# Reordering a two-layer hybrid decoder step: first stage by sets of chunks, pages and weights a stage ahead, linear attention without GpSimd products, key copies ahead of scalings

## The reference

```python
x = layer_norm(x)                                   # 1088 rows of 1024
for l in range(2):
    shift1, scale1, gate1, shift2, scale2, gate2 = split(silu(c) @ w_ada[l] + b_ada[l], 6)   # 9 rows c
    h = x * (1 + scale1) + shift1
    gq, gk, gv, gg, glr, lx, lgate, dq, dkv, kr = split(h @ w_in[l])
    o_gla = rms_norm(gla(gq, gk, gv, log_sigmoid(glr @ w_gate + b) / 16)) * silu(gg)   # chunked linear attention
    o_lru = gelu(lgate) * rg_lru(causal_conv(lx))                                      # a scan over the tokens
    q = rms_norm(dq) @ w_uq; q_lat = q_nope @ w_uk                                     # latent attention, 8 heads
    keys = concat(past_ckv[page_table], rms_norm(dkv)), concat(past_kr[page_table], rope(kr))
    o_mla = softmax(q_lat @ keys_c.T + rope(q_rope) @ keys_r.T, causal) @ keys_c @ w_uv
    x = layer_norm(alpha * x + gate1 * (concat(o_gla, o_lru, o_mla) @ w_out[l]))
    h2 = x * (1 + scale2) + shift2
    x = layer_norm(alpha * x + gate2 * ((silu(h2 @ w_g) * (h2 @ w_u)) @ w_down))
```

## Time and profile before

| | |
|---|---|
| median of 3 runs | 3480.62 us (3478.95 to 3488.6) |
| the profiled execution, its own time | 3485.3 us |
| its span, first to last instruction | 3483.5 us |
| TensorE busy | 3255.1 us (93%) |
| VectorE busy | 2326.5 us (67%) |
| ScalarE busy | 1587.2 us (46%) |
| GpSimd busy | 202.9 us (6%) |
| mean granted TensorE clock | 0.966 |

### The profile page before, as it was taken

How to read it: one execution, slowest core, us unless ns; L and a number is a source line. 1 busy time by engine, 2 the same in 40 slices (tenths; PEclk the granted TensorE clock), 3 DMA queues, 4 the chain that set the end, 5 groups by cost and what they waited for, 6 DMA issues and landing times. The chain is left out here.

```text
span 3483.5 us, 61376 instructions
## 1 busy us (share of the span) xinstructions
PE 3255.1 (93%) x23676; PEld 2738.1 (79%) x23676; DVE 2326.5 (67%) x4390; ACT 1587.2 (46%) x3159; POOL 202.9 (6%) x254
## 2 busy tenths in 40 slices
PE   6988898998999999999989889989989999999997
PEld 4875566776998998999978655667769899899997
DVE  5254665444488889888844456644446888888878
ACT  5343554444255454444344445634433554544432
POOL 0020111110000000000001111011100000000000
PEclk9998999998999999999989889999989999999998
DMA  7026102443033332222121340044421333322231
GB/s 272 27 93 230 66 1 105 164 157 106 16 106 96 95 101 80 90 87 86 52 109 31 137 142 1 1 163 165 158 49 52 94 98 96 94 87 83 91 106 57
DMA packets 158149, 334.72 MB, mean 96 GB/s; under 512 B 18556, under 2 KB 85406, under 8 KB 146471
## 3 DMA queue, kind: packets, MB, share of 16 engines
q1 hardware_dynamic: 146342, 246.91, 22.2%
q0 software_dynamic: 11520, 83.89, 6.8%
HBM read 315.32 MB, written 15.43 MB: 95 GB/s over the span
## 5 line engine op out<-in xcount | busy, mean ns | idle before, releaser
L2494 ACT CAST w_ffn_hi<-w_ffn 128x512 fp32r<-128x512 f32 x616 | 371.3, 618 | 259.4 <-DVE w_ffn L2676 128.0
L445 PE MATMUL psum<-h_lo,w_ffn_hi 128*128 128x256 f32 (+1 forms) x1408 | 406.6, 289 | 0.0
L2688 DVE TENSOR_TENSOR w_ffn_lo<-w_ffn,w_ffn_hi 128x1024 fp32r<-128x1024 f32 (+1 forms) x366 | 383.0, 1047 | 11.8 <-ACT w_ffn_hi L2494 11.7
L444 PE MATMUL psum<-h_forms_hi,w_ffn_hi 128*128 128x288 f32 x1232 | 364.1, 296 | 3.4 <-DVE w_ffn_lo L2688 3.4
L446 PE MATMUL psum<-h_forms_hi,w_ffn_lo 128*128 128x288 f32 x1232 | 363.7, 295 | 0.0
L444 PE MATMUL psum<-h_hi,w_ffn_hi 128*128 128x256 f32 x1232 | 348.6, 283 | 10.9 <-DVE w_ffn_lo L2688 9.1
L444 PE MATMUL psum<-ffn_act_hi,w_down_hi 128*128 128x288 f32 (+1 forms) x992 | 332.3, 335 | 21.1 <-DVE w_down_lo L2694 6.5
L446 PE MATMUL psum<-h_hi,w_ffn_lo 128*128 128x256 f32 x1232 | 346.8, 281 | 0.0
L446 PE MATMUL psum<-ffn_act_hi,w_down_lo 128*128 128x288 f32 (+1 forms) x992 | 326.6, 329 | 0.0
L445 PE MATMUL psum<-ffn_act_lo,w_down_hi 128*128 128x288 f32 (+1 forms) x992 | 325.9, 328 | 0.0
L430 DVE SCALAR_TENSOR_TENSOR xT<-psum,adaT,xT 128x512 f32<-128x512 f32 (+2 forms) x320 | 191.1, 609 | 130.4 <-PE psum L446 127.0
(11 more groups left out here) (450 smaller groups left out, 7624.8 us busy)
## 6 DMA issues: line engine op xcount, KB each, us to landing
w_ffn<-in_w_gu SPq DMA_DIRECT2D x352, 256.0 KB, 2.6
w_ada_pair<-in_w_ada SPq DMA_DIRECT2D x40, 1024.0 KB, 6.1
w_down<-in_w_down SPq DMA_DIRECT2D x192, 192.0 KB, 2.4
residual_kept<-xT SPq DMA_DIRECT2D x2, 4352.0 KB, 19.2
xT<-residual_kept SPq DMA_DIRECT2D x2, 4352.0 KB, 14.2
w_ada_first<-in_w_ada SPq DMA_DIRECT2D x4, 2048.0 KB, 22.2
w_out<-in_w_out SPq DMA_DIRECT2D x16, 512.0 KB, 7.3
w_in_T<-in_w_in_T SPq DMA_DIRECT2D x12, 512.0 KB, 4.4
```

Of the source, the lines that this page charges most:

```text
L444: pe.matmul(o, wh, xh, start=first, stop=False)
L445: pe.matmul(o, wh, xl, start=False, stop=False)
L2494: act.copy(WGH[:, (j + 1) % NR].bitcast(F32R), WGR[:, m % 2, i]).then_inc(s_wh, 1)
L2688: dve.tensor_tensor(WGL[:, m % 2, i:i + n].bitcast(F32R), WGR[:, m % 2, i:i + n], WGH[:, r:r + n], ALU.subtract).then_inc(s_wl, n)
```

## The change

Start and input: the transposes run column group by column group and start when three row blocks are normalised, through four banks; the weights of the modulation come in 1 MB loads so that each set j holds shift and scale of chunks 2j and 2j+1, and vectors and modulation go set by set. Most of the constants are loaded, and the page indices computed, in the input stage. `w_in_B` is loaded in the stage before (in layer 1: at the end of layer 0's feed-forward part), and in layer 0 the split of k = 0 is made there too.

```diff
+            gg = [(c, n) for n in range(3) for c in range(KD)]
+            def back_bank(g):
+                return bank(4 + g % 4)
...
                     for j, (g0, g1) in enumerate(STAGES):
+                        pe.wait_ge(nm, min(NBLK, 3 * j + 3))
                         for g in range(g0, g1):
                             back(g)
+                            if j and g == g0 + 3:
+                                rows_turned(j - 1)
+                        ada(j)
+                    rows_turned(2)
+                    ada(3)
+                    rows_turned(3)
...
+                    sp.wait_ge(tb, len(gg))
+                    for k in range(KD):
+                        sp.dma_start(WBR[:, k], of("w_in_B", 0)[:, k]).then_inc(s_wb[k > 0], 16)
...
-                    for k in range(KD):
+                    for k in range(k_0, KD):
+                        act.copy(wbh(k).bitcast(F32R), WBR[:, k]).then_inc(s_bh, 1)
                         act.copy(HIN[:, k].bitcast(F32R), HT[:, k]).then_inc(s_hh, 1)
-                        act.wait_ge(s_wb[k], 16)
-                        act.copy(wbh(k).bitcast(F32R), WBR[:, k]).then_inc(s_bh, 1)
```

```diff
-        ADA_PER_STEP = {24: (1, 2, 3, 3, 3, 3, 3, 3, 2, 1), 16: (1, 2, 2, 2, 2, 2, 2, 2, 1, 0)}
+        ADA_PER_STEP = {24: (2, 3, 3, 3, 3, 3, 3, 2, 1, 1), 16: (2, 2, 2, 2, 2, 2, 2, 1, 1, 0)}
+        MIXED_AT = (2, 3)
...
-                    for c in range(2):
-                        pool.tensor_tensor(HT[:, 2 + c], LG[:, c], XC[:, c], ALU.mult).then_inc(s_mx, 1)
...
+                            for q in todo[:1] if s == 1 else ():
+                                pair(q)
                             if s + 1 < NBLK:
                                 cumulate(s + 1)
-                            for q in todo[:1]:
+                            for q in todo[:1] if s > 1 else ():
                                 pair(q)
                             attend(s - 1)
...
+                        if s in MIXED_AT:
+                            c = MIXED_AT.index(s)
+                            dve.tensor_tensor(HT[:, 2 + c], LG[:, c], XC[:, c], ALU.mult).then_inc(s_mx, 1)
```

```diff
-            for hp in range(1, HP):
-                for j in range(NPJ):
-                    pj_at.setdefault((hp - 1) * PER + 5 + j, []).append((hp, j))
+            SPREAD = {hp: (5, 8, 9, 10, 11, 12, 13, 14, 15, 16) if hp == 1 else (1, 4, 5, 8, 9, 10, 12, 13, 14, 15)
+                      for hp in range(1, HP)}
+            for hp, at_items in SPREAD.items():
+                for j, x in enumerate(at_items):
+                    pj_at.setdefault((hp - 1) * PER + x, []).append((hp, j))
...
+                    page_rows(pool, 0).then_inc(s_pf, 16)
+                    rope_rows(pool, 0).then_inc(s_pf, 16)
...
+                        for hp, j in pj_at.get(i, []) if i > 4 else ():
+                            read(hp * NPJ + j)
                         if i:
                             scale(i - 1)
...
-                        for hp, j in pj_at.get(i, []):
+                        for hp, j in pj_at.get(i, []) if i <= 4 else ():
                             read(hp * NPJ + j)
```

```diff
+                @block.sync
+                def _(sp):
+                    sp.wait_ge(s_v, NS - 2)
+                    sp.wait_ge(s_s, NS - 1)
+                    for k in range(NPRE):
+                        sp.dma_start(wo(k)[0][:, 0:KD - 1], w_out_rows(k)[:, 0:KD - 1]).then_inc(s_ow[k], 16)
...
                     keys(0)
-                    pe.wait_ge(s_na, 1)
+                    new_turned()
                     pe.wait_ge(s_ql, 1)
-                    for s in range(NS):
+                    for s in range(NS - 1):
                         scores(s)
-                        if s + 1 < NS:
-                            keys(s + 1)
+                        if s == 0:
+                            new_values()
+                        keys(s + 1)
...
-                    values(NS - 1)
+                    scores(NS - 1)
+                    values(NS - 2)
                     pe.wait_ge(s_mx, NS)
                     pe.transpose(bank(0)[0:SB, 0:P], NMR[:, :, NCH], ident).then_inc(s_fp, 1)
+                    turn(NS - 1)
...
+                    values(NS - 1)
                     pe.wait_ge(s_f, 3)
```

```diff
                     for k in range(KD):
-                        pe.wait_ge(s_xl, k + 1)
-                        pe.wait_ge(s_ol, k + 1)
+                        if k:
+                            pe.wait_ge(s_xl, k)
+                            pe.wait_ge(s_ol, k)
...
-                            act.wait_ge(s_om, 3 * KD if j == NR - 1 else 2 * KD)
-                        act.copy(WGH[:, (j + 1) % NR].bitcast(F32R), WGR[:, m % 2, i]).then_inc(s_wh, 1)
+                            act.wait_ge(s_om, (2 * KD, KD + 10, KD + 10, KD + 12, KD + 12, 3 * KD)[j])
+                        act.copy(WGH[:, (j + 1) % NR].bitcast(F32R), wg(WGR, m, i)[:, 0]).then_inc(s_wh, 1)
```

More of the change, by code:

```diff
@@ L599, in t_end @@
                 return at_item[("T", j, 2)] + 1
-            s_wb = [sem(f"w_in_B_{k}_in") for k in range(KD)]
+            s_rest = sem("consts_in")
+            k_0 = 1 if layer[0] == 0 else 0
+            s_fa = sem("first_pairs_in")
             s_wa, s_wt, s_p = sem("w_in_A_in"), [sem(f"w_in_T_{i}_in") for i in range(3)], sem("params_in")
@@ L1002, in _ @@
                         scan(c)
+                    for b in range(SB if layer[0] == 0 else 0):
+                        dve.tensor_scalar(IDX[:, b, 0:NCH], bc(PT[:, b], NCH), float(2 * NCH), None, ALU.mult)
+                        lk(dve.tensor_scalar(IDX[:, b, NCH:NCH + 1], PT[:, b:b + 1], 2.0, None, ALU.mult))
+                        lk(dve.tensor_tensor(IDX[:, b, :], IDX[:, b, :], IBASE, ALU.add))
                 @block.gpsimd
@@ L1071, in stage_gla @@
             s_az = sem("ada_bank_zero")
-            pairs = range(M_G1 // 2 if layer[0] == DEPTH - 1 else 0, ADA_PAIRS)
+            pairs = ada_pairs()
             PARTS = [(0, 4), (4, 7), (7, NBLK)]
@@ L2188, in build, with wg, wo, wo_hi @@
         assert C_SM + 4 + 2 * D <= C_N
+        def wg(parts, m, i, n=1):
+            i0, _, w = next(x for x in parts[m % 2] if x[0] <= i and i + n <= x[1])
+            return w[:, i - i0:i - i0 + n]
+        def wo(k):
+            return WOR[:, k // 4, :, k % 4], WOL[:, k // 4, :, k % 4]
+        def wo_hi(k):
+            return WOH[:, :, k]
+        def w_out_rows(k):
+            return of("w_out")[:, k].rearrange("p (c n) -> p c n", n=P)
         def row_in_h(blk):
```

472 lines of the change are left out of this document (289 added, 183 removed).

## The result

The changed kernel takes 3391.86 us (median of 4 runs, 3388.07 to 3396.17), the one before 3479.78 us beside it: a ratio of 0.9744, 95% interval 0.9721 to 0.9766, 88 us less where 68 were forecast. Run again later it took 3383.35 us (5 runs), ratio 0.9718 (0.970 to 0.9736). The result lies inside the forecast range (3382 to 3446), 20 us under the forecast of 3412, and at the figure of the clock rival, 3391. Its profiled execution has a span of 3394.1 us, of which TensorE is busy 3231.4 (95%).

What follows compares the result with a forecast made beforehand. TensorE, busy 93% of 3483.5 us, was taken as the bound, so only its idle or lower-clock time could be won. Seam by seam savings summed to 68.4 us, taking the 3480.6 median to 3412, range 3382 to 3446.

Steps and rivals of the forecast that it cites:

- the clock rival: Whole kernel, mainly linear attention: fewer holes also mean fewer stretches at 1.2 GHz, 21 us more, 3391 us; chance 0.19.
- The sum: Whole kernel: seam by seam savings, 7 + 0.9 + 14 + 16 + 14 + 16.5 = 68.4 us.
- Start and input, 7 us: First stage to first input product: early transposes, modulation by sets, weights ready; 8.4 less 1.4, range 5 to 9.5.
- the early transposes: First stage: half a block of transposes moves ahead, before all rows are normalised, saving 2 us.
- Linear attention, 7 each: Each layer: without GpSimd's products beside VectorE, the 6.8 us hole shrinks to about 1.3; 7 us, range 1 to 16.
- 1.6 in each: Linear attention, each layer: some 1.6 us of doubled time at the lower clock behind the hole shrinks with it.
- Prompt attention, 8 each: Each layer: key and query copies ahead of ScalarE's scaling, with spread positions, remove TensorE's waits; 8 us, range 0 to 12.
- The prompt rival: Prompt attention gives nothing, as scaling and turn are late in place of the copy; 3428 us, chance 0.14.
- Entry and exit of decode, 10.9 each: Decode, each layer: 7 us at the entry and 3.9 from the shortened chain and split copies at the tail.
- the 7 forecast: Entry to decode, each layer: prefetched page keys first, new values behind the scores; 7 us, range 4 to 9.
- the 10.3: Exit from decode and output stage, layer 0: shorter tail and output weights and split made ahead; range 8 to 12.
- Output stage, 6.4 and 2.3: Output product: 6.4 us in layer 0 from weights and split ahead, 2.3 in layer 1 from splits after the gains.

Runs made afterwards that it cites:

- one: Changed kernel with the two gate-by-scan products of linear attention back on GpSimd and off VectorE; 3393.76 us, ratio 0.9755.
- three: Changed kernel with ScalarE's reads of the projections behind the scaling again in prompt attention, positions still spread; 3397.1 us, ratio 0.9742.
- four: Changed kernel with prompt attention's projections at their old steps 5 to 14, ScalarE still reading them ahead of the scaling; 3397.94 us, ratio 0.9754.
- seven: Changed kernel with page 0 and its rope rows fetched at the start of the decode stage again; 3402.74 us, ratio 0.9776.
- eight: Changed kernel with w_out 0 to 3 loaded and the k = 0 operands split in the output stage again; 3398.58 us, ratio 0.976.
- run two: Kernel before, with only the two gate-by-scan products of linear attention moved from GpSimd to VectorE; 3459.84 us, ratio 0.9942.
- eleven: Changed kernel with the first stage's small turning products late and no-effect products in linear attention's two 1.3 us holes and four further places; 3372.7 us, ratio 0.9701.
- ten: Kernel before, with 24 small extra products of no effect in linear attention's 6.8 us hole; 3475.0 us in 11 runs, ratio 0.9981.

## Why the prediction was right, and where it was off

**The sum.** 68.4 us forecast, 65.7 and 68.0 us of idle time saved. The sum was right as a sum over holes, and off as a forecast of the time because it counted 3 us for the clock, which gave 21 and 35.

**Start and input, 7 us.** Idle time fell by 8.6 and 7.0 us, the early transposes by their 2.7. The term was right for the holes, but the lower clock, for which I took off 1.4 with the kept rows, cost 9.8 us more than before in the first profile and 2.9 in the second. In runs one, three, four, seven and eight, which share this stage, the linear stage began at 231.7 to 232.5 us, 6 us earlier than the 238.2 of before, against 237.3 and 235.3 in the two profiles of the changed kernel.

**Linear attention, 7 each.** The step is right: 5.56 to 1.17 us, hole 1.39 (1.3 forecast). The first of the 1.29 us products is hidden: it runs at 253.75, in a stretch (250.0 to 266.7) in which TensorE is busy 16.70 of 16.70 us. Idle time saved 7.5 and 6.0 in the first profile. What failed is the size of the clock's part: in layer 1 15.8 and 13.0 us came back in the two profiles, in layer 0 -1.5 and 4.7, against 1.6 in each. In layer 1 all eleven profiles with the new order of pairs lost 2.7 to 9.7 us, the two with the old order and the products on GpSimd 17.4 and 18.9, and run two 7.8; in layer 0 they scatter on both sides of before (4.9 to 19.8 against 9.5 to 11.9). The forecast had this as a rival, with the stretches as its reason, and weighed it at 0.19.

**Prompt attention, 8 each.** The waits on the key copy are gone. Idle time saved is 7.3 and 11.6 in the first profile, 9.0 and 11.5 in the second; in layer 1 a wait of 2.3 us for weights went too, and in layer 0 one of 3.4 came in the first profile and of 1.7 in the second. The two causes were weighed the wrong way: the prediction has the copy's place ahead of the scaling first and the spread as what keeps it safe; of the 9.2 us of waits that went in each layer the spread alone does 7.7 and the order alone 5.6. The prompt rival is out, no new wait on the scaled probabilities came (0.5 us at most, as before).

**Entry and exit of decode, 10.9 each.** 14.9 and 15.1 us. Idle time saved 7.9 in each, 3 less than forecast, and 7 us from the clock in each (10.2 and 10.4 to 3.4 and 3.3), which the prediction left out here. By seams, in layer 0: from the last product of the stage before to the second step's first scores (563.99 to 590.37 before, 547.88 to 564.84 after) idle time fell from 9.8 to 4.3 us, 5.5 of the 7 forecast; from the last but one values to the first output product (835.63 to 862.75, 810.21 to 824.96) from 14.2 to 4.9, 9.3 of the 10.3. The clock's part stays at 2.2 to 5.8 us in every kernel with the new decode stage, and at 7.5 to 10.4 in the three with the old one, so it goes with the change. It lies at the two ends: before, TensorE worked 8.0 and 3.4 us at 1.2 GHz at the entry (564.0 to 577.7, 581.1 to 584.5) and 3.4 and 5.6 at the tail (840.5 to 843.9, 847.4 to 856.1), half of which is the 10.2; after, 3.4 at each end. Seven and eight bring back waits of 5.6 to 8.5 us at either end, and the loss stays at 3.1 to 3.8. That does not show that the clock holds through them: in seven TensorE is idle in most of the slow stretch, and in eight the stretch (817.8 to 828.0 in layer 0) lies behind the end of the decode stage. Whether the shorter waits or the new order of the work did it is open.

**Output stage, 6.4 and 2.3.** 5.9 and 1.0 in the first profile; idle time 6.2 and 2.1, as forecast.

**The clock rival.** It named the amount, 21 us, and the place in part: of the clock time regained in the first profile, 14.3 us net are in linear attention and 13.9 in decode, less 9.8 lost at the start. That its 21 is so near the first run is luck: the second profile gave back 35. Its reason, fewer holes, fits the ends of decode but is not shown, and it does not cover the rest. The rule it was set beside, "TensorE: Matmul & The Clock Gate", section "HAM oscillation — how this bites in real kernels" of the Trainium skill, is that idle gaps between bursts drop the clock. The trace agrees in part at run seven's gaps of 8.3 and 8.5 us: both run into or lie in a stretch at 1.2 GHz, which begins 2 us inside the gap in layer 1 (2200.8), but 1.7 us ahead of it in layer 0 (541.9). It does not agree at 38.0 us in the changed kernel, where the clock falls behind 10.00 of 10.00 busy us, nor at 253.9 in eleven, with gaps of at most 0.60 us. What does decide when this stream of small products falls stays open; a profile of the same instructions differed by 14.5 us.

## What to carry to other kernels

Sum idle time of the bounding engine hole by hole, and forecast the clock apart from it: here the first repeats within 3 us and the second moves by 15 between two profiles of one kernel. A clock loss counted on busy time also looks small when the engine merely waits through the slow stretch, so look at the granted clock around the wait too. Judge an edit worth under 10 us by the idle time of its stage rather than by the kernel's time. Look for a small VectorE operation that takes five times its usual time: here it was what ran on GpSimd beside it, and moving that alone was worth 19 us of 3480, about half of it idle time.

## What the runs showed of the hardware

VectorE's four 32x128 products took 5.55 to 5.58 us beside GpSimd's two products in the three kernels that had them there (before, one and ten), and at most 1.17 us in all others. Stretches of 13.7 to 27.3 us in which TensorE was never idle ran at 1.2 GHz in linear attention in nine of the fourteen profiles, at other times in most. A first page by index took 8.3 to 8.5 us of waiting when asked for at the start of a stage. Extra products of no effect, 1.2 to 5.5 us in a hole, cost nothing measurable.
